# Three places of an instruction order moved in a two-layer hybrid backbone: a norm sum behind a weight tile, a bias load ahead of a weight load, and attended values ahead of the next scores

## The reference, cut to what matters

```
u = hx @ w_in                      # conv | rwkv | lora gate | attention q,k,v | merge gates
zd = z + mu[d] * (shift(z, d) - z) # per direction d; r, k, v, lw, la are its parts
w  = exp(-exp(-softplus(-(w0 + tanh(lw) @ w2)) - 0.5));  a = sigmoid(a0 + la @ a2)
kk = k * k_k / norm(k * k_k);  k = k * (1 + (a - 1) * k_a)
S  = S * w + (S @ -kk) (kk * a) + v k;  y = S @ r       # scan over the tokens
bonus = sum(r * k * r_k) * v
s  = q k^T / 8 + bias(rpb), windowed | q kc^T / 8;  c_x = softmax(s) @ [v | vc]
y_x = sum_n(sigmoid(gate_n) * (branch_n @ w_up_n)) @ w_o;   FFN: (silu(a) * b) @ w_out
```

## Time and profile before

| | |
|---|---|
| median of 3 runs | 3591.43 us (3591.18 to 3594.68) |
| profiled execution, its own time | 3591.43 us |
| its span, first to last instruction | 3589.7 us |
| PE busy | 3324.9 us, 93% |
| DVE, ACT, POOL busy | 43%, 33%, 23% |
| prologue, block 0 of layer 0 begins | 178.51 us |
| attention of layer 0 | about 978 to 1232 us |
| prologue, block 0 of layer 1 begins | 2171.19 us |
| attention of layer 1 | about 2853 to 3031 us |

### The profile page before, as it was taken

How to read it: one execution, slowest core, us unless ns; L and a number is a source line. 1 busy time by engine, 2 the same in 40 slices (tenths; PEclk the granted TensorE clock), 3 DMA queues, 4 the chain that set the end, 5 groups by cost and what they waited for, 6 DMA issues and landing times.

```text
span 3589.7 us, 78540 instructions
## 1 busy us (share of the span) xinstructions
PE 3324.9 (93%) x33764; PEld 2605.6 (73%) x33764; DVE 1525.7 (43%) x2844; ACT 1169.0 (33%) x2475; POOL 826.4 (23%) x520
## 2 busy tenths in 40 slices
PE   6999999999999998899999789999999988889998
PEld 4777777777777787788888566666766666658886
DVE  3445454554355552200044454646464355430033
ACT  4333333332333433311112343333332344342222
POOL 1211110111122222122223122111111232324453
PEclk9999999999999999999999899999999999999999
DMA  5433333343355441111111133323233243422322
GB/s 193 126 98 109 109 105 108 98 121 124 99 183 158 157 151 57 46 60 64 64 53 59 59 104 107 90 78 91 76 107 101 87 127 123 152 65 94 99 88 76
DMA packets 246697, 364.84 MB, mean 102 GB/s; under 512 B 154096, under 2 KB 155376, under 8 KB 245888
## 3 DMA queue, kind: packets, MB, share of 16 engines
q1 hardware_dynamic: 226976, 294.57, 27.0%
q10 hardware_dynamic: 14976, 35.66, 2.5%
q0 software_dynamic: 4448, 30.24, 2.4%
HBM read 291.20 MB, written 69.21 MB: 100 GB/s over the span
## 4 chain that ended last, share of the span: by engine, by line
PE 78%; DVE 6%; issue 5%; ACT 5%; DVEq 2%; POOLq 1%; DMA 1%; POOL 1%; SPq 1%; PEld 0%; ACTq 0%; PEldq 0%
PE banks L278 21%; PE banks L279 17%; PE banks L280 17%; PE banks L1569 3%; PE banks L947 3%; PE banks L1556 2%; PE banks L1565 2%; PE banks L1524 1%; PE banks L386 1%; POOLq L2282 1%; PE banks L1578 1%; DVE arena L587 1%; POOL slot_rounded L857 1%; PE banks L1920 1%; PE banks L502 1%
## 5 line engine op out<-in xcount | busy, mean ns | idle before, releaser
L278 PE MATMUL banks<-hx_rounded,branch_weights_high 128*128 128x256 f32 (+1 forms) x1312 | 528.3, 403 | 72.4 <-DVE resid_rounded L536 20.6
L280 PE MATMUL banks<-hx_rounded,slot_rounded 128*128 128x512 f32 (+1 forms) x1624 | 577.0, 355 | 0.0
L278 PE MATMUL banks<-hx_high,weight_parts 128*128 128x512 f32 (+1 forms) x1560 | 556.1, 356 | 18.6 <-DVE hx_low L536 18.1
L857 POOL TENSOR_TENSOR slot_rounded<-slot,branch_weights_high 128x512 fp32r<-128x512 f32 x188 | 241.9, 1308 | 1423.1 <-ACT branch_weights_high L852 1421.8
L279 PE MATMUL banks<-hx_low,weight_parts 128*128 128x512 f32 (+1 forms) x1560 | 555.5, 356 | 0.0
L280 PE MATMUL banks<-hx_high,weight_parts 128*128 128x512 f32 (+1 forms) x1560 | 553.6, 355 | 0.0
L279 PE MATMUL banks<-resid_rounded,branch_weights_high 128*128 128x256 f32 (+1 forms) x1312 | 466.2, 355 | 0.0
L278 PEld LDWEIGHTS banks<-hx_rounded,branch_weights_high 128*128 128x128 f32 x1312 | 253.3, 193 | 157.5 <-issue 98.7
L280 PEld LDWEIGHTS banks<-hx_rounded,slot_rounded 128*128 128x128 f32 x1624 | 313.7, 193 | 44.4 <-issue 0.2
L278 PEld LDWEIGHTS banks<-hx_high,weight_parts 128*128 128x128 f32 x1560 | 295.9, 190 | 67.7 <-issue 22.2
L280 PEld LDWEIGHTS banks<-hx_high,weight_parts 128*128 128x128 f32 x1560 | 295.7, 190 | 42.4
(11 more groups left out here) (240 smaller groups left out, 5802.4 us busy)
## 6 DMA issues: line engine op xcount, KB each, us to landing
slot<-in_w_mix SPq DMA_DIRECT2D x120, 512.0 KB, 4.0
slot<-in_w_ffn_in SPq DMA_DIRECT2D x88, 512.0 KB, 3.5
arena<-chunk_inputs SPq DMA_DIRECT2D x48, 640.0 KB, 4.2
arena<-in_w_ada SPq DMA_DIRECT2D x50, 512.0 KB, 4.3
slot<-in_w_ffn_out SPq DMA_DIRECT2D x44, 512.0 KB, 3.5
slot<-in_w_ada SPq DMA_DIRECT2D x40, 512.0 KB, 3.7
chunk_inputs<-arena SPq DMA_DIRECT2D x80, 256.0 KB, 3.3
arena<-side_projections POOLq DMA_DIRECT2D x16, 1152.0 KB, 6.2
```

Of the source, the lines that this page charges most:

```text
L278: first = nc.tensor.matmul(out, w_hi, x_hi, start=start, stop=False)
L280: return first, nc.tensor.matmul(out, w_lo, x_hi, start=False, stop=stop)
L857: last = nc.gpsimd.tensor_tensor(slots_r[g % 3][:, half], slots[g % 3][:, half], weights_high(g)[:, half], ALU.subtract)
```

## The change

Three edits of order. No operation is added or removed.

1. Prologue: `bonus_sum(1)` comes after tile 7 instead of after tile 6. SP's stores of direction 1 are split: k where all four stood, then the load of tile 10, then r, a, b and the staged load of block 0.
2. Attention: SP's load of tile 47 comes after the bias load of pair 1 and after the row loads of tile 44, in place of ahead of both. (The bound of the loop is written otherwise, g + 3 < NT; tiles 48 to 59 are loaded where they were.)
3. Attention: the weighted sum of unit p comes before the scores of unit p + 2.

```
@@ sync_program
-                tile_load(sp, l, NRW + 3)
                 for hp in range(HP):
                     if hp + 1 < HP:
                         sp.wait_ge(a_bias.sem, a_bias.ready(l, hp))
...
-                        if NRW < g < NT - 3:
+                        if g + 3 < NT:
                             tile_load(sp, l, g + 3)
@@ stage_pe, steps(), prologue
                     yield from tile(6)
+                    yield from tile(7)
                     yield from bonus_sum(1)
-                    for t in range(7, 11):
+                    for t in range(8, 11):
                         yield from tile(t)
@@ stage_sp, prologue
                     if t == 7:
-                        for o in range(1, 5):
+                        store(1, 1)
+                    if t == 8:
+                        for o in (2, 3, 4):
                             store(o, 1)
                         stage_load(hq, 0)
                     next_load(t)
@@ attn_pe
                     pe.wait_ge(u_trc[l].sem, u_trc[l].ready(0, hp, p + 1))
+                    weighted(p)
                     if p + 2 < len(ps):
                         scores(p + 2)
-                    weighted(p)
                     fill(hp, 4 + 2 * p)
```

## The result

| | median us | lowest to highest | runs |
|---|---|---|---|
| before | 3591.43 | 3581.61 to 3594.68 | 5 |
| after | 3614.21 | 3610.11 to 3615.04 | 5 |

The ratio is 1.0062 (95% interval 1.0046 to 1.008): 22.8 us slower between the medians. The forecast was 3618.5 us with a range of 3605 to 3629, so direction and range held, and the sum of 27.2 us was 4.4 us too large. The profiled execution of after took 3615.32 us (span 3613.5), against 3591.43 (span 3589.7).

The account below looks back on a forecast made before the run. PE, 93% busy and in order, was taken to bound the kernel, so each edit counted by PE's waits. 3591.4 + 11.5 + 10.8 + 4.9 = 3618.6, said as 3618.5 us; range 3605 to 3629.

Parts of the forecast that it names:

- The four waits: PE before block 0, about 6 us (layer 0), 8 (layer 1); ACT at tile 47, 9; layer 1's copy, 1 more per pair.
- Rival A: Layer 0's attention: ACT isn't caught on tile 47, so edit 2 is free; total 3607.8 us; chance 0.09.
- rival C: Attention: only the scores' delay is hidden, so edit 3 costs nothing; total 3613.7 us; chance 0.08.
- rival D: Prologue: tile 10's earlier load removes PE's waits, 7.0 us faster if other edits are free; 3584.4 us; chance 0.03.
- Rival B: Layer 0's prologue: staging delay small because stores land faster; edit 1 costs only about 4 us, total 3611; chance 0.08.
- Edit 1, layer 0: Prologue: block 0 starts at 184.3 instead of 178.51, 5.8 us of wait, plus 1.8 us for the lower clock.
- Edit 1, layer 1: Prologue: b's stores end at 2168.1 instead of 2164.22, adding 3.9 us to PE's 4.40 us wait; no clock term.
- Edit 2, layer 0: Attention: tile 47's load goes twenty us later; PE waits 9.0 us for ACT's copy, plus 1.8 for clock: 10.8 us.
- Edit 2, layer 1: Attention: tile 47's load goes at about 2866, hidden in ACT's idle time until 2872.98: 0, up to 1.5 us.
- Layer 1's 4.4: Attention: the scores' delay reaches PE through ACT's copy at one unit in each of four pairs, 1.1 us per pair.
- Layer 0's 0.5: Attention: more filling lies between and PE has no wait at its scores, so edit 3 costs only 0.5 us.
- A fixed 1.8 us per such stall: Layer 0, prologue and attention: half of 3.86 us lost at the 1.2 GHz level after a new PE wait.

Follow-up runs that it names:

- edit 2 alone: Only the load of tile 47 moved behind the bias load and the row loads, against before: median 3599.80 us, mean 10.8 ± 1.4 us more.
- the runs of edit 3: Against before, weighted sum ahead of scores: both layers 10.6 ± 1.3 us more, layer 0 only 3.5, layer 1 only 3.1; scores amid the sum 5.1.
- the split alone: Only SP's stores split around tile 10's load, bonus sum still ahead of tile 7, against before: median 3598.86 us, mean 7.9 ± 1.9 us more.
- k early: Before with k of direction 1 stored at t = 6, ahead of tile 9's load: median 3589.13 us, mean 1.4 ± 1.4 us more.

## Why the prediction was right, point by point

**Bounds and mechanism.** The four waits it named are in the trace, with the releasers it named, and at both large ones PE's offset rose by about the wait: 4.3 us for the 4.15 in after, 8.8 for the 8.79 of edit 2 alone. Rival A (edit 2 free) falls with the 9.03 us wait, rival C (the scores' delay hidden) with the runs of edit 3, rival D with the split alone: tile 10's load came earlier there and nothing was gained. Rival B, a small delay in layer 0, was right in kind: the stores did land sooner behind their last issue, and layer 0 came out 1.7 us below its term, where B had all of edit 1 at 4.

**Edit 1, layer 0: 7.6 us forecast, 5.9 measured** (0.3 to 6.2 on the offsets). Bonus at 167.5: 167.60. The row copy ahead of b at 172.9: 173.13. b made at 175.2: 175.32. Last store at 177.0: 176.63. Then the step that was mis-sized: the staged load was to leave 3.4 us after the stores' issue, as in before, and left 2.4 us after it (179.03). That gap was 3.4 and 3.1 us behind eight stores in a row (before, layers 0 and 1), 2.8 and 2.6 behind the split's six in a row, and 2.4 wherever the last stores had waited for b; why is not shown. The wait is thus 4.15 instead of 5.8 us. PE's 3.9 us from that issue were 4.0, and the clock cost 1.6 us, 1.8 forecast (offset 4.3 at block 0, 5.9 behind it, both less the 0.3 that the trace starts with). The text's r and a "between 170 and 174" had the right time with half of the reason: r's values were made at 170.55, and tile 10's load, which the text left out of the queue, went at 170.00.

**Edit 1, layer 1: 3.9 forecast**, 3.0 more wait (7.37 against 4.40). The 4.0 us on the offsets agree with it by luck: 1.4 of them are clock ahead of the edit, and 2.5 are left. The same step was mis-sized: the gap behind the last store was 2.4 us instead of 3.1. The edit as a whole: 11.5 forecast, 7.2 ± 1.9 measured.

**Edit 2, layer 0: 10.8 forecast, 10.8 measured** in the first pair of edit 2 alone (0.2 to 11.0), with a wait of 8.79, or 9.03 in after, against 9.0. The landing was 6.3 and 6.55 us where 6.4 was taken. The Trainium skill's fit ("DMA: Bandwidth & Descriptors", Anatomy of one DMA — SWDGE (gpsimd) path), which as an estimate gave 3.2 us for the landing and 5.8 for the wait, lies below both. It was made for single transfers issued from GpSimd; this load goes from SP 0.4 us behind a row load, so these runs show that it does not carry over to this place and do not test the fit itself.

**Edit 2, layer 1: 0 forecast, about 2 measured** (3.94 and 3.54 us of wait against 1.97). This step failed. Its issue time was right (2866 was said, and 2886.78 less the 21.1 of offset is 2865.7), but the load took 7.9 us to land instead of 6.4, and I had set it against 2872.98, when ACT next did anything. In between stands the rounding itself, which before's ACT had started at 2867.96 and behind which the next operation starts 0.96 us later: the tile was needed by 2872.0, not by 2873. With a landing of 6.4 us it would have come 0.1 us late; with 7.9 us it came 1.5 us late, and PE's wait grew by 1.6 (edit 2 alone) and 2.0 us (after). The prediction's upper bound of 1.5 us was a little too low.

**Edit 3: 4.9 forecast, about 7 to 8 measured** (8.2 ± 1.2 in its place, 3.5 and 3.1 by layer). Layer 1's 4.4 stands within the errors: 3.9 us of waits, 3.1 ± 2.1 in the mean. Layer 0's 0.5 failed; it is 3.1 to 3.7. I looked only for waits at the scores and missed that the same exponentials stand ahead of the evictions on ACT, whose waits grow by 2.7 us.

**The sum.** Two terms were too large, by 1.7 and 1.4 us, and two too small, by 2 and 3. That the sum came within 4.4 us is thus in part luck. The traced stretches give 29.5 us, and the total is 22.8. Some 5.5 us come off in the merge and the norm. It was tempting to say that waits there absorb them, but from the end of layer 1's attention to the end of the kernel 10 of the 13 kernels gain on before's trace, k early by 3.7 us: before's profiled execution was slow there. In layer 0's the kernels range from -3.7 to +3.5; whether part of the delay is absorbed stays open.

## What to carry to other kernels

When a load moves back, take the time at which its consumer needs it from the consumer's own start (the rounding), not from the next busy row, and look at what waits in the queue ahead of it: one load that waits for a slot or a bank delays all behind it. A delay on an in-order engine reaches every instruction behind it, so list all that somebody else waits for, evictions included, not only the one on the path. Two halves of an edit can each cost the whole; only running both halves shows it.

## What the runs showed of the hardware

A 512 KB load took 6.3 to 6.6 us from issue to ACT's start in layer 0's attention, behind two row loads, and 7.1 to 7.9 in layer 1's. In the window of edit 2 alone, 2872 to 2880 us, the software queue, on which POOL's loads go, moved as much as the hardware queue with SP's (packets, MB, share of the engines):

```profile
q1 hardware_dynamic: 574, 1.09, 41.2%
q0 software_dynamic: 193, 1.09, 36.6%
```

That the two slow each other down is not shown.

The granted clock after the new waits, of after: the stretch, its length, busy times by engine, then the clock, 1.00 being the 2.4 GHz level.

```profile
160.00:183.00 23.00, 18.47 (x114) 15.08 (x112) 5.75 (x8) 3.86 (x6) 5.84 (x5) 1.00 0.65 191
183.00:190.00 7.00, 6.94 (x84) 5.89 (x84) 2.81 (x6) 1.94 (x8) 0.00 (x0) 0.76 0.38 120
190.00:200.00 10.00, 10.00 (x176) 7.98 (x176) 3.18 (x12) 2.06 (x4) 1.75 (x2) 1.00 0.25 85
```
```profile
1021.40:1035.00 13.60, 13.24 (x127) 10.10 (x127) 6.80 (x17) 2.51 (x6) 1.70 (x2) 0.81 0.38 131
```

After 4.15 us of idle time the clock costs 0.24 of 7 us, 1.7 us; after 9.03 us 0.19 of 13.6 us, 2.6. A fixed 1.8 us per such stall was close for the first and 0.8 us below the second; the offsets of edit 2 alone give 2.0 us for it (0.2 to 11.0, less the wait of 8.79).

Executions of one and the same kernel differ more than most terms here: 98 runs of before lie between 3580 and 3606 us, with a standard deviation of 4.6. Waits of the same place agree between profiles to some tenths of a microsecond (8.79 and 9.03, 7.24 and 7.37), the totals only to several.
